# The low half of a weight split made by a DMA that adds, in a two-layer hybrid decoder kernel

## The reference

```python
def hybrid_layer(x, ...):
    h = rms_norm(x, norm_g)
    u = h @ w_in
    c_q, c_kv, k_pe, g_mla, u_conv, g_conv, z, xbc, dt_raw = jnp.split(u, offs, axis=-1)
    o_mla = mla_mixer(c_q, c_kv, k_pe, ...) * jax.nn.silu(g_mla)
    o_conv = conformer_conv_mixer(u_conv, ...) * jax.nn.silu(g_conv)
    o_ssd = ssd_mixer(z, xbc, dt_raw, ...)     # ends in rms_norm(y * jax.nn.silu(z), norm_g)
    y = jnp.concatenate([o_mla, o_conv, o_ssd], axis=-1) @ w_out
    return x + y
```

## Time and profile before

| | |
|---|---|
| median of three runs | 1618.69 us |
| the profiled execution's own time | 1618.13 us |
| its span, first to last instruction | 1616.0 us |
| PE busy | 1552.6 us, 7062 matmuls |
| DVE busy | 1031.9 us, 1528 instructions |
| ACT busy | 652.0 us, 983 instructions |
| POOL busy | 44.6 us, 86 instructions |
| DMA | 158.12 MB, a mean of 98 GB/s |
| granted TensorE clock, mean | 0.988 |

### The profile page before, as it was taken

One profiled execution on the slowest core, in us unless ns is written; L12 is line 12 of the kernel. 1 busy time (PEld: TensorE's weight loads), 2 busy tenths in 40 slices (PEclk: granted clock), 3 DMA queues, 4 the chain that ended last, 5 costly groups with the idle time before them and its releaser, 6 DMA issues.

```text
span 1616.0 us, 18431 instructions
## 1 busy us (share of the span) xinstructions
PE 1552.6 (96%) x7062; PEld 1236.3 (77%) x7062; DVE 1031.9 (64%) x1528; ACT 652.0 (40%) x983; POOL 44.6 (3%) x86
## 2 busy tenths in 40 slices
PE   6999999999998999999999999999999899999997
PEld 5877777777776777888877877777777678778885
DVE  6545764889898776543455457668998985673231
ACT  6445443334444534211244455433444444351110
POOL 0000000000000000101000000000000000001100
PEclk9999999999999999999999999999999999999999
DMA  5322232222233313445422223211122232225441
GB/s 216 92 92 87 79 92 66 78 66 66 75 103 99 102 59 101 150 138 156 137 98 75 91 79 103 80 66 66 66 78 85 95 108 85 80 89 166 145 140 65
DMA packets 44423, 158.12 MB, mean 98 GB/s; under 512 B 5521, under 2 KB 5809, under 8 KB 44337
## 3 DMA queue, kind: packets, MB, share of 16 engines
q1 hardware_dynamic: 36720, 129.64, 24.6%
q0 software_dynamic: 6464, 23.12, 5.0%
q10 hardware_dynamic: 1152, 4.19, 0.7%
HBM read 148.50 MB, written 8.44 MB: 97 GB/s over the span
## 4 chain that ended last, share of the span: by engine, by line
PE 79%; DVE 11%; ACT 5%; issue 2%; DMA 1%; DVEq 0%; SPq 0%; POOL 0%; ACTq 0%; POOLq 0%
PE acc L491 17%; PE acc L493 17%; PE acc L492 17%; PE S L496 5%; PE S L491 4%; PE S L492 4%; PE S L493 4%; PE T L493 2%; PE T L492 2%; PE T L491 2%; DVE wlo L998 2%; ACT whi L744 2%; DVE xb L989 2%; PE O L496 2%; PE T L631 1%
## 5 line engine op out<-in xcount | busy, mean ns | idle before, releaser
L491 PE MATMUL acc<-hhi,whi 128*128 128x512 f32 (+1 forms) x1504 | 605.5, 403 | 22.9 <-DVE wlo L998 22.9
L998 DVE TENSOR_TENSOR wlo<-stage,whi 128x1024 fp32r<-128x1024 f32 (+3 forms) x252 | 300.5, 1197 | 470.1 <-ACT whi L744 468.3
L493 PE MATMUL acc<-hhi,wlo 128*128 128x512 f32 (+1 forms) x1504 | 591.2, 393 | 0.0
L492 PE MATMUL acc<-hlo,whi 128*128 128x512 f32 (+1 forms) x1504 | 591.1, 393 | 0.0
L744 ACT ACTIVATE whi<-stage 128x1024 fp32r<-128x1024 f32 (+3 forms) x252 | 259.6, 1035 | 487.0 <-PE acc L493 270.5
L491 PEld LDWEIGHTS acc<-hhi,whi 128*128 128x128 f32 (+1 forms) x1504 | 284.7, 189 | 87.0 <-DVE wlo L998 25.0
L493 PEld LDWEIGHTS acc<-hhi,wlo 128*128 128x128 f32 (+1 forms) x1504 | 284.1, 189 | 62.9
L492 PEld LDWEIGHTS acc<-hlo,whi 128*128 128x128 f32 (+1 forms) x1504 | 284.9, 189 | 61.8 <-issue 3.3
L1046 DVE SCALAR_TENSOR_TENSOR cacc<-glu,pv,cacc 128x512 f32<-128x512 f32 x240 | 171.7, 749 | 4.5
L491 PE MATMUL S<-hhi,whi 128*128 128x512 f32 x192 | 75.5, 393 | 0.0
L493 PE MATMUL S<-hhi,wlo 128*128 128x512 f32 x192 | 74.7, 389 | 0.0
(11 more groups left out here) (229 smaller groups left out, 1592.5 us busy)
## 6 DMA issues: line engine op xcount, KB each, us to landing
stage<-weights SPq DMA_DIRECT2D x236, 512.0 KB, 3.4
y_features<-xg POOLq DMA_DIRECT2D x32, 256.0 KB, 4.2
acsb<-acs_rows POOLq DMA_DIRECT2D x16, 384.0 KB, 4.1
xg<-x_features ACTq DMA_DIRECT2D x8, 512.0 KB, 11.2
xr<-x_features POOLq DMA_DIRECT2D x16, 256.0 KB, 4.2
xr<-y_features POOLq DMA_DIRECT2D x16, 256.0 KB, 4.1
stage<-weights SPq DMA_DIRECT2D x8, 256.0 KB, 2.6
stage<-weights SPq DMA_DIRECT2D x4, 384.0 KB, 3.0
```

Of the source, the lines that this page charges most:

```text
L491: nc.tensor.matmul(out, a, c, start=start, stop=False)
L492: nc.tensor.matmul(out, a, d, start=False, stop=False)
L493: return nc.tensor.matmul(out, b, c, start=False, stop=stop)
L998: nc.vector.tensor_tensor(wlo[u % RING][:, 0:w], stage[u % STAGE][:, 0:w], whi[u % RING][:, 0:w].bitcast(F32), ALU.subtract).then_inc(lo_d ...
```

## The change

1. VectorE's `split` is gone. ScalarE writes after whi a second copy of the stage buffer with scale -1 into wlo, which is rounded in the same way, so wlo holds -whi. POOL waits for it (`neg_done`) and issues a DMA that reads the weights of the unit a second time from DRAM and adds them onto wlo (`accum_op`). TensorE waits for that DMA, on one of three semaphores, instead of for VectorE. A stage buffer is free at `neg_done`.
2. The other DMAs leave POOL: the residual rows and stores go to SP's queue, each behind a stage load, the sums go to ScalarE's (`acs_rows`, `acsb`). The load of the sums for the next chunk is issued when ScalarE has taken its six rows of the last; the one for the first chunk is issued in the last step of attention. The last four stores of a layer stand behind the first four stage loads of the next.
3. The gates gmla, gconv and z use ScalarE's Silu of the whole input. For gmla and gconv its result is the gate; for z VectorE multiplies it in. The gates of the convolution input (ug) and the scan's inputs keep tanh.
4. The first four units of a layer are quarters of both tiles (4 values of k, both tiles) instead of halves of one, so tiles 0 and 1 use one unit at a time. At the start of the kernel the splits stand at k = 1, 4 and 8, the last four k and the squares of x one step later each.

```diff
-    for half in range(2):
-        s.append(("first", (half,), [unit("in", 0, half), unit("in", 1, half)]))
+    for quarter in range(4):
+        s.append(("first", (quarter,), [unit("in01", quarter)]))
...
         @block.gpsimd
+            def add_weights(layer, u):
...
+                pool.wait_ge(neg_done.sem, neg_done.at(layer, u + 1))
                 pool.sem_inc(pool_go, 1)
+                pool.dma_start(wlo[u % RING][:, 0:WIDTHS[u]], weight_rows(layer, u),
+                               accum_op=ALU.add).then_inc(lo_loaded[u % RING].sem, 16)
+
+            for u in range(RING):
+                add_weights(0, u)
             for layer in range(DEPTH):
                 for name, args, own in STEPS:
+                    for u in own:
+                        add_weights(layer, u + RING)
...
         @block.tensor
-                        pe.wait_ge(lo_done.sem, lo_done.at(layer, u + 1))
+                        pe.wait_ge(lo_loaded[u % RING].sem, lo_loaded[u % RING].at(layer, 16 * (u // RING + 1)))
...
         @block.scalar
                     nc.scalar.activation(whi[u % RING][:, 0:w], stage[u % STAGE][:, 0:w], ACT.Copy).then_inc(hi_done.sem, 1)
+                    nc.scalar.activation(wlo[u % RING][:, 0:w], stage[u % STAGE][:, 0:w], ACT.Copy,
+                                         scale=-1.0).then_inc(neg_done.sem, 1)
...
-                        if kind in ("gmla", "ug", "gconv", "z"):
+                        if kind == "ug":
                             tanh()
+                        if kind in ("gmla", "gconv", "z"):
+                            tanhs[0] += 1
+                            gate = temp2[:, :] if kind == "z" else xg[:, i if kind == "gmla" else 6 + i, :]
+                            act.wait_ge(tanh_in.sem, tanh_in.at(layer, tanhs[0]))
+                            a(tanh_done, gate, temp[:, :], ACT.Silu)
...
+                        if n == 25:
+                            act.wait_ge(acs_stored.sem, acs_stored.at(layer, 16))
+                            act.wait_ge(o_taken.sem, o_taken.at(layer, HEADS))
+                            sums_load(0)
...
         @block.vector
-                    dve.wait_ge(hi_done.sem, hi_done.at(layer, u + 1))
-                    w = WIDTHS[u]
-                    nc.vector.tensor_tensor(wlo[u % RING][:, 0:w], stage[u % STAGE][:, 0:w],
-                                                       whi[u % RING][:, 0:w].bitcast(F32), ALU.subtract).then_inc(lo_done.sem, 1)
```

More of the change, by code:

```diff
@@ L167 @@
 NU = len(UNITS)
-TILE_UNIT = [UNITS.index(("in", j, 1)) for j in range(len(TILES))] + [UNITS.index(("out2", 3))] * 2
+TILE_UNIT = [UNITS.index(("in01", 3))] * 2 + [UNITS.index(("in", j, 1)) for j in range(2, len(TILES))] + [UNITS.index(("out2", 3))] * 2
 TILE_UNIT += [UNITS.index(("out", f, 1)) for f in range(2, KX)]
@@ L432, in _ @@
                         sp.dma_start(pvn[:, :], params[layer * P + P:layer * P + 2 * P, :]).then_inc(params_loaded.sem, 16)
+            for f in range(KX - 4, KX):
+                store(DEPTH - 1, f)
+            sp.wait_ge(x_stored.sem, x_stored.at(DEPTH - 1, 16 * KX))
             sp.wait_ge(params_loaded.sem, params_loaded.at(DEPTH - 1, 0))
@@ L465, in _ @@
[L465 to L478, removed]
@@ L511, in _ @@
                     for u in own:
-                        pe.wait_ge(lo_done.sem, lo_done.at(layer, u + 1))
+                        pe.wait_ge(lo_loaded[u % RING].sem, lo_loaded[u % RING].at(layer, 16 * (u // RING + 1)))
                     if name == "first":
-                        half = args[0]
-                        if layer and half == 0:
+                        quarter = args[0]
+                        if layer and quarter == 0:
                             pe.wait_ge(acc_taken.sem, acc_taken.at(layer - 1, len(TILES) + KX - 2))
-                        for k8 in range(8):
-                            k = 8 * half + k8
+                        for k4 in range(4):
+                            k = 4 * quarter + k4
                             pe.wait_ge(h_lo.sem, h_lo.at(layer, k + 1))
                             for j in range(2):
-                                last = three(in_bank(j)[:, :], *w(own[j], k8 * P, P), hhi[:, k, :], hlo[:, k, :],
-                                             k == 0, k == KX - 1)
-                                if k8 == 7:
-                                    last.then_inc(unit_used.sem, 1)
+                                last = three(in_bank(j)[:, :], *w(own[0], (2 * k4 + j) * P, P), hhi[:, k, :],
+                                             hlo[:, k, :], k == 0, k == KX - 1)
+                        last.then_inc(unit_used.sem, 1)
                     elif name == "in":
@@ L791, in _ @@
                     if name == "first" and args == (0,) and layer == 0:
+                        for k in range(12, KX):
+                            x_hi_loaded(k)
+                    if name == "first" and args == (1,) and layer == 0:
                         for k in range(KX):
@@ L1064, in _ @@
                     half_taps(0)
-                    for k in range(KX):
-                        if k in (1, 2, 8):
-                            split((1, 2, 8).index(k))
+                    for k in range(12):
                         x_lo(k, 0)
@@ L1116, in _ @@
                 for name, args, own in STEPS:
-                    for u in own:
-                        split(u + RING)
                     if name == "first" and args == (0,) and layer == 0:
+                        for k in range(12, KX):
+                            x_lo(k, 0)
+                    if name == "first" and args == (1,) and layer == 0:
                         for k in range(KX):
@@ L1409, in host_weights @@
             block = rows(blocks)
+        elif kind == "in01":
+            block = np.concatenate([rows(w_in[:, k:k + 1, :, TILES[j][2][0][0]:TILES[j][2][0][0] + P])
+                                    for k in range(4 * args[0], 4 * args[0] + 4) for j in range(2)], axis=2)
         elif kind == "v":
```

117 lines of the change are left out of this document (67 added, 50 removed).

## The result

The changed kernel takes **1770.57 us** (median of four runs, 1764.31 to 1776.45) against 1618.26 for the kernel before beside it: a ratio of 1.0938, 95% interval 1.0892 to 1.0983. The forecast was 1644, its range ended at 1695. The direction was right, the size was not: 152 us slower instead of 26. The profiled execution took 1766.84 us with a span of 1765.0.

The account below looks back on a forecast made before the run. TensorE's matmuls were taken as the floor, so only its waits counted. Losses of 58.8 us less gains of 32.5 gave +26.3 on 1618.1, forecast 1644 us, range 1600 to 1695.

Parts of the forecast that it names:

- rival 3: SSD stage: ScalarE takes over as the limit, half or more of 18 us won is lost, 1653 to 1662; chance 0.10.
- (a): After projections: both slots return at once, the next unit is short by 2.6 us, six times, 15.6 us lost.
- (b): At 588 us, split after the conv branch: TensorE's gap 8.6 us instead of 3.12, twice 5.5, 11.0 us lost.
- (c): At 649 us, split behind the last branch inputs: ready 4.6 us after TensorE wants it, twice, 9.2 us lost.
- what comes: the way of a low half: Rounding, negation, POOL's issue, adding DMA: landing 5.6 us, low half ready 6.9 us after its rounding ended.
- (d): At 105 us, ScalarE late behind the rotated key: low half short by 2.0 us, twice, 4.0 us lost.
- (e): Kernel start: first matmul near 17.5 us for 12.2, a later unit ready near 53; 9 us lost in all.
- no cost in the output stage: Output stage: 9.56 us of room exceeds the 6.9 needed, no loss while the landing stays under 8.3 us.
- (f): Several units with 7 us of room, around pointwise units and second splits after a projection: 0.3 us each, 3 lost.
- Rival 2: The ring sets the pace: above a landing of 8.3 us every unit waits; about 1740, or 1700 us; chance 0.12.
- (g): TensorE's granted clock falls after the new gaps, as to 0.83 after the earlier 3.12 us gap: 7 us lost.
- 16 us per us of landing: The loss at the places where TensorE waits for low halves changes about 16 us per us of landing.

Follow-up runs that it names:

- the kernel with the subtraction: The changed kernel with VectorE's subtraction making the low halves again, all else of the change kept: 1597.61 us, ratio 0.9875 to the kernel before.
- The late wait: The changed kernel, but in a projection TensorE waits for the second unit only at the third product, its first use: 1729.23 us.
- The output kernel: VectorE's subtraction for all units except 97 to 125 (output stage), which use the adding DMA; otherwise as the kernel with the subtraction: 1637.84 us.
- both edits: The changed kernel with the negated copy made before the rounded one and a projection's second unit awaited only at its third product: 1681.41 us.

## Why the prediction was wrong

The direction was right. What failed is the sum of the losses, 58.8 us: the landing and the stops behind it, the heads of the projections, which were not in it, and the clock.

**Right.** The gains by VectorE's relief: I had 5.1 + 10.0 + 4.4 + 3.4 + 2.3 = 25.2 us for mt, xb, kr, prob and xg; TensorE stood 17.5 less in the SSD stage, 3.4 less in attention, and kr's 4.4 are gone, 25.3. ScalarE did not become the limit there (rival 3). The places (a), (b), (c) and the start are where the stops came. The plain landing of 5.0 was the measured 4.9. The residual rows and stores on SP's queue cost nothing, as forecast: with the subtraction the output stretch is 158.9 us in both layers, for 157.8 and 158.9. The Silu gates, put at nothing, gained about 6 us in the kernel with the subtraction; in the changed kernel they were not tried alone.

**Step "what comes: the way of a low half", mis-sized.** I took 5.6 us for the landing and measured 7.6. The 5.0 of its plain part was right; the add was mis-sized, 0.6 us where 2.7 were measured (7.6 against 4.9, both with the stage load beside them). Its packets take twice as long (0.335 for 0.163 us a packet). My own 6.6, the destination counted like another 512 KB, was nearer; my reason for going below it, that POOL's 4.2 us was of the busiest stage, did not hold. What I had also left out is that the negation frees the stage buffer too, so SP's load starts with the adding DMA on the same engines; without it the add lands 1.9 us earlier. The order alone showed that: both wait for `neg_done`. The Trainium skill says of DMAs issued from SP, ACT and GpSimd that "they all run on the same 16 DMA engines and interleave" ("DMA: Bandwidth & Descriptors", Rules for kernel authors), and the 1.9 us agree. What the Trainium skill says of the add in a ReduceScatter, that its two source reads halve the rate ("Collectives: The Full Stack", The bandwidth ceiling), agrees with the time of this case's packets, 0.328 against 0.174 us.

**Step (a), mis-sized and a place missed.** Behind the projections TensorE stood 36 us, not 15.6, the six gaps 5.6 to 6.2: there two adds and their loads run at once, and the landing is 8.5 to 8.9 us. At 170 us of the changed kernel:

```profile
159.43 1.06 ACT L745 ACTIVATE whi<-stage 128x1024 fp32r<-128x1024 f32 x1 [15.37 <-PE M L494]
...
162.01 0.86 POOL L477 DMA_DIRECT2D wlo<-weights  x1 [16.52 <-ACT wlo L746]
...
170.94 0.80 PE L492 MATMUL acc<-hhi,whi 128*128 128x512 f32 x1 [6.02 <-DMA wlo<-weights]
```

for the earlier trace rows. The heads of the projections, another 32.7 us, were not in the sum at all: I had measured the room of the second unit up to its first use, not up to the wait that TensorE executes for it. The late wait removes them.

**Steps (b) and (c).** 16.9 and 18.7 us for 11.0 and 9.2. After the convolution's norm, for the earlier trace rows, and at (c):

```profile
651.27 0.80 PE L492 MATMUL acc<-hhi,whi 128*128 128x512 f32 x1 [11.68 <-DMA wlo<-weights]
...
727.53 0.80 PE L492 MATMUL acc<-hhi,whi 128*128 128x512 f32 x1 [9.47 <-DMA wlo<-weights]
```

At (b) two units are split one right behind the other, so two adds run together (landings 8.8 and 9.4); that makes the 3 us per place that I lacked. At (c) the landing is 8.7 and the gaps are 9.47 and 9.23. The landing is 3 us of what I lacked there; for the rest TensorE stood 0.8 us before the DMA was issued, where my reading of the earlier trace rows had it come about 1 us after, so it did not come only "as much earlier" as the split. Step (d) was too dear: 1.05 and 0.24 us, where I had 4.0.

**Step (e), the start.** First matmul at 20.6 for 17.5 forecast, the DMA landing in 10.1 us at a DMA share of 0.93. With the second stop, at 56, and the second layer TensorE stood 16.8 us longer, for 9.

**Step "no cost in the output stage".** It has a condition, a landing under 8.3, and the condition failed: the landings there have a median of 8.0 us, 22 of the 52 of units 100 to 125 are over 8.3 (the longest 10.3), at a DMA share of 0.96, and at 15 of 56 units TensorE stands 0.1 to 1.8 us. With the dearer units around the pointwise product it is 22 us, where (f) had 3. The output kernel shows 40 us for the whole stage, (c)'s stops among them. Rival 2 described this, but made it all or nothing; in fact only the longer landings are over the mark.

**Step (g), the clock.** I had 7 - 3 = 4 us; TensorE was busy 38.8 us longer. The kernel with the subtraction has a mean clock of 0.996, the changed one 0.955. Each of a layer's three projections has a stop at its head and one behind it, with 18 to 22 us of work between stops, and the granted clock over the 145 us from 140 to 285 is 0.85. This error and the missed heads of the projections are the two largest, and the one follows from the stops of the other: with the late wait the clock of the window is 0.92, with both edits 0.95.

**The last store.** 1.6 us forecast from medians of landing; 7.6 measured. The end of the program behind POOL's store took 9.4 us, behind SP's 2.4, and the landing is 0.3 of that: the rest is POOL's DRAIN. That was to be seen in the tail of the trace before, and I had priced it with another row.

**The slope.** "16 us per us of landing" was the sum's own check and was false by more than twice: 41 for the first microsecond. It counts only the places that the sum had: not the six heads of the projections, and not the units of the output stage, more of which wait with each microsecond. The clock is no part of it, as TensorE's busy time stayed.

## What to carry to other kernels

Measure the room for a slower producer up to the instruction that waits for it, not to the first use, and price each handover together with whatever else the same semaphore sets off. A detour that takes work off a busy engine belongs only where its whole way, with neighbours in flight, is shorter than the ring's room: here the same DMA gains 25 us in two stages and loses 133 in two others, and choosing by stage beats both kernels. When a term is set between two estimates, ask what speaks for going below the dearer one. Where stops come in close succession, add the clock that they take: here TensorE's busy time grew by a third of what its standing grew (38.8 and 117.7 us).

## What the runs showed of the hardware

- An adding DMA onto SBUF takes 0.33 us per 4 KB packet from HBM and 0.34 from SBUF, against 0.17 for a plain one from HBM (medians), and 0.86 us of POOL's time per issue against 0.53.
- A 512 KB adding DMA lands in 4.5 us from SBUF, 5.4 from HBM, 7.3 to 7.6 with one 512 KB load beside it, 8.5 to 10.6 with two pairs or under the start's traffic. A plain one from POOL, with a load beside it, lands in 4.9. Why the source in HBM costs 0.9 us at equal packet times stays open.
- The end of the program came 9.4 us after the last store's issue on POOL and 2.4 after that on SP, though both stores landed in 2.0 to 2.3 us. The rest on POOL is its closing DRAIN of 6.8 us; what that does is open.
- Table loads take 1.283 us each. 26 more of them at a ScalarE busy share of 43% cost less than 32 products saved on VectorE gave.
